# bf16 copies of two weights in DRAM, and a seven-product stage three steps deep, in a hybrid decoder layer

## What is computed

```python
hcat = x @ w_in                                  # conv inputs B, C, h and retention q, k, v, g
y_conv = b_gate * causal_short_conv(c_gate * hc, conv_w)
o = chunkwise_retention(rotary(q), rotary(k) * 128**-0.5, v)
y_ret = silu(g) * head_group_norm(o, ret_gn_w, ret_gn_b)
mix = concat([y_conv, y_ret], -1) @ w_out
x = layer_norm(2**0.25 * x + mix, ln1_w, ln1_b)
ff = square(relu(x @ w_ff1)) @ w_ff2             # 1024 -> 4096 -> 1024
ple = sigmoid(x @ w_ple_gate) * (p @ w_ple_proj)
x = layer_norm(2**0.25 * x + ff + ple, ln2_w, ln2_b)
```

## Time and profile before

| | us |
|---|---|
| median of 6 runs | 813.43 (810.13 to 848.31) |
| the profiled execution | 814.77 |
| span of its slowest core (core 1), all rows from here | 813.2 |
| spans of its cores 0 to 7 | 800.2, 813.2, 800.4, 807.7, 810.1, 803.0, 808.8, 802.8 |
| busy on core 1: PE, DVE, ACT, POOL | 763.5, 545.4, 305.7, 181.5 |

### The profile page before, as it was taken

The page is one execution under the profiler, slowest core; times in us unless marked ns, Lnnn a source line. Parts: engine busy times, 40 slices in busy tenths (PEclk is TensorE's granted clock), DMA queues, the critical chain, the costliest instruction groups (busy, mean ns, idle before and its releaser), DMA issues.

```text
span 813.2 us, 12342 instructions; the slowest of 8 cores (800.2 to 813.2 us)
## 1 busy us (share of the span) xinstructions
PE 763.5 (94%) x3896; PEld 357.5 (44%) x3896; DVE 545.4 (67%) x762; ACT 305.7 (38%) x624; POOL 181.5 (22%) x209
## 2 busy tenths in 40 slices
PE   3999999999999999999969999999898889999994
PEld 1444455555555454444424444454343334444441
DVE  4565855458865888785438876916777667756667
ACT  2222225655466236655522000125665562200431
POOL 9000036563454311120010000000444440000011
PEclk9999999999999999999989999999999999999997
DMA  9997040601115575799999956591595658186422
GB/s 129 167 177 158 27 130 4 102 15 39 53 53 156 89 119 207 174 297 264 213 213 158 227 218 127 170 322 52 167 297 184 210 155 282 54 156 130 138 95 105
DMA packets 31025, 122.65 MB, mean 151 GB/s; under 512 B 3696, under 2 KB 5872, under 8 KB 24560
## 3 DMA queue, kind: packets, MB, share of 16 engines
q0 software_dynamic: 9360, 39.85, 30.6%
q1 hardware_dynamic: 20736, 80.43, 28.2%
q10 hardware_dynamic: 864, 1.57, 0.8%
HBM read 122.89 MB, written 38.80 MB: 199 GB/s over the span
## 4 chain that ended last, share of the span: by engine, by line
PE 74%; DVE 9%; DMA 8%; issue 4%; POOL 2%; ACT 2%; DVEq 0%; SPq 0%; ACTq 0%; POOLq 0%
PE ps L189 72%; DMA s_w<-ring_105 3%; DMA xT_56<-xT 2%; PE ps L193 2%; DVE xacc L207 2%; DVE ps L196 1%; DVE ycat L196 1%; DMA ring_108<-s_w 1%; DMA ring_109<-s_w 1%; POOL lnst L196 1%; DVE lnst L729 0%; DVE eb_132 L196 0%; DVE xacc L196 0%; ACT tR_140 L218 0%; ACT hT L218 0%
## 5 line engine op out<-in xcount | busy, mean ns | idle before, releaser
L196 DVE TENSOR_TENSOR xacc<-xacc,ps 128x512 f32<-128x512 f32 x80 | 53.1, 685 | 53.5 <-PE ps L189 52.0
L196 POOL TENSOR_TENSOR lnst<-lnst,neghalf 128x1 f32<-128x1 f32 x32 | 32.3, 1011 | 245.2 <-DVE lnst L200 194.5
L189 PE MATMUL ps<-ring_106,ycat 128*128 128x512 bf16 x256 | 61.9, 390 | 5.3 <-DVE hT L196 5.3
L189 PE MATMUL ps<-ycat,ring_108 128*128 128x512 bf16 x208 | 49.8, 387 | 4.2 <-DVE ps L196 2.2
L189 PE MATMUL ps<-ycat,ring_109 128*128 128x512 bf16 x208 | 49.1, 384 | 4.0 <-DMA ring_109<-s_w 2.2
L189 PE MATMUL ps<-ring_104,ycat 128*128 128x512 bf16 x224 | 51.4, 379 | 0.0
L218 ACT ACTIVATE ycat<-ps 128x1024 bf16<-128x1024 bf16 x16 | 16.3, 1021 | 90.6 <-PE ps L193 87.7
L196 DVE TENSOR_TENSOR ycat<-hT 128x2048 bf16<-128x2048 bf16 x36 | 43.4, 1222 | 1.5
L189 PE MATMUL ps<-ycat,ring_106 128*128 128x512 bf16 x176 | 42.0, 385 | 0.0
L189 PEld LDWEIGHTS ps<-ring_106,ycat 128*128 128x128 bf16 x256 | 25.4, 100 | 36.6 <-issue 9.0
L189 PE MATMUL ps<-ring_105,ycat 128*128 128x512 bf16 x160 | 37.3, 379 | 0.3 <-DVE ra_80 L196 0.3
(11 more groups left out here) (348 smaller groups left out, 1589.0 us busy)
## 6 DMA issues: line engine op xcount, KB each, us to landing
out<-xacc SPq DMA_DIRECT2D x14, 512.0 KB, 2.9
s_w<-ring_104 SPq DMA_DIRECT2D x10, 512.0 KB, 10.0
s_w<-ring_105 SPq DMA_DIRECT2D x10, 512.0 KB, 12.6
xtmp<-x SPq DMA_DIRECT2D x8, 512.0 KB, 5.2
ring_106<-w_ff POOLq DMA_DIRECT2D x4, 1024.0 KB, 11.0
ring_108<-w_ff POOLq DMA_DIRECT2D x4, 1024.0 KB, 12.5
ring_109<-w_ff POOLq DMA_DIRECT2D x4, 1024.0 KB, 15.8
s_x1f<-xtmp SPq DMA_DIRECT2D x8, 512.0 KB, 10.1
```

Source lines behind the costliest of these rows:

```text
L189: self.P.op("pe", lambda e: e.matmul(out, lhsT=lhsT, rhs=rhs, start=start, stop=stop, skip_group_check=skip), reads, writes)
L196: self.P.op(eng, lambda e: e.tensor_tensor(out=out, in0=in0, in1=in1, op=op), reads, writes)
```

## The change

Three things are changed.

1. Ten DRAM-to-DRAM copies (`copy_bf16`) cast the eight slabs of `w_ff1` and the two of `w_gate` to bf16 in a new scratch tensor `s_wb`, on POOL's queue, one at the end of each step t = 1 to 10 of the retention loop. `load_slab` then loads these slabs from `s_wb`, still on POOL's queue. `gen_w1` no longer stores `M3` and `M4`; `load_pieces` takes them from `s_wb`.
2. `phase_ff1_last` is reordered so that a stage spans three steps: M2, M3, M1 of n, M6 of n-1, M7 of n-2, M5 and M4 of n-1. Banks: r in 0 to 2, t in 3 to 5, p in 6 and 7. `eb` has names of its own, and the slab ring 3 gets new ones afterwards. `load_pieces` stands at other places; the first gate slab's prefetch moves from n = 12 to n = 14.
3. `gen_out` becomes one generator `gen_outs` for all eight blocks, two steps per block: statistics of b, then the output of b-1; the reload of b-1, then the two norm operations of b. One step is issued per stage from n = 2. There is no flush before the second gate: what is left runs in the gate, whose loop steps it until the block it needs has been reloaded.

```diff
-    s_w1 = nc.dram_tensor("s_w1", [4, 7, 128, 4, 512], BF16).ap()
+    s_w1 = nc.dram_tensor("s_w1", [4, 5, 128, 4, 512], BF16).ap()
+    s_wb = nc.dram_tensor("s_wb", [10, 128, 8, 512], BF16).ap()
...
-            h.dma("pool", ring[i][:], wsrc[nm][g], ("ring", i), [], r)
+            src, rd = wsrc[nm][g], []
+            if nm in ("ff1", "gate"):
+                k = g + 8 * (nm == "gate")
+                src, rd = s_wb[k], [("s_wb", k)]
+            h.dma("pool", ring[i][:], src, ("ring", i), rd, r)
+
+        def copy_bf16(k):
+            h.dma("pool", s_wb[k], w_ff1[k] if k < 8 else w_gate[k - 8], ("wc", k // 4, k % 4), [],
+                  [("s_wb", k)])
...
+            if 1 <= t <= 10:
+                copy_bf16((0, 4, 1, 5, 2, 6, 3, 7, 8, 9)[t - 1])
...
-            for m, (t, r) in (("M3", a[0]), ("M4", b[1])):
-                h.dma("sp", s_w1[g, W1.index(m)], t, ("st",) + r[0], r, [("s_w1", g, m)])
...
-                return [(3 * n + k) % 8 for k in range(3)]
+                return n % 3, 3 + n % 3, 6 + n % 2
...
+            def stage(n, split=False):
+                if not split:
+                    first(n)
+                if n >= 3:
+                    last_sums(n - 2)
+                first_sums(n)
+                if n == 0:
+                    xsum("M6")
+                if n == 1:
+                    xsum("M7")
+                if n % 4 == 3:
+                    load_pieces(n // 4 * 7 + 13)
+                if n >= 2:
+                    product(n - 1, "M6", banks(n - 1)[2], True)
+                    sq6 = relu(banks(n - 1)[2])
+                if n >= 2:
+                    product(n - 2, "M7", banks(n - 2)[0], True)
+                    sq7 = relu(banks(n - 2)[0])
+                keep(n)
+                if n >= 2:
+                    square(n - 1, 1, 1, sq6, "act")
+                    square(n - 2, 0, 0, sq7, "pool")
+                if n % 4 == 1 and n > 1:
+                    load_pieces((n // 4 - 1) * 7 + 17)
+                if n >= 2:
+                    bg.step()
+                if n >= 1:
+                    r, t, p = banks(n - 1)
+                    product(n - 1, "M5", t, True)
+                    product(n - 1, "M4", r, True)
+                    sq5, sq4 = relu(t), relu(r)
+                    square(n - 1, 1, 0, sq4, "act")
+                    square(n - 1, 0, 1, sq5, "pool")
+                if n % 4 == 0 and n > 0:
+                    load_pieces((n // 4 - 1) * 7 + 16)
...
-                if n == 12:
+                if n == 14:
                     prefetch(17)
...
+                    while s_ == 1 and loaded[0] <= b:
+                        bg.step()
...
+        def gen_outs():
+            for b in range(9):
+                if b < 8:
+                    g = gen_ln(xacc[:, b, :], ("xa", b), lnt[2], lnt[3], "ln2w", "ln2b", b)
+                    next(g)
+                if b > 0:
+                    h.dma("sp", out[(b - 1) * 128:b * 128, :], xacc[:, b - 1, :], ("outq", b - 1),
+                          [("xa", b - 1)], [("out", b - 1)])
+                    outs.append(("out", b - 1))
+                yield
+                if b > 0:
+                    h.dma("sp", xacc[:, b - 1, :], s_x1f[(b - 1) // 4, ((b - 1) % 4) * 128:((b - 1) % 4 + 1) * 128, :],
+                          ("xl", b - 1), [("s_x1f", 7 + b)], [("xa", b - 1)])
+                    loaded[0] = b
+                if b < 8:
+                    for _ in g:
+                        pass
+                    yield
...
-            bg.flush()
+            if s_ == 0:
+                bg.flush()
```

More of the change, by code:

```diff
@@ L412, in build_nc @@
     xtmp = at("xtmp", [128, 8, D], F32, o_w4, [("xt", b) for b in range(8)])
-    eb = [at("eb%d" % i, [128, 512], F32, o_gs + i * 2 * KB, None) for i in range(4)]
+    eb = [at("eb%d" % i, [128, 512], F32, o_gs + i * 2 * KB, ("eb", i)) for i in range(4)]
+    for k in range(2):
+        P.place(("ring", 3, k, 1), o_gs + k * 4 * KB, o_gs + (k + 1) * 4 * KB)
     xs4 = at("xs4", [128, 4, 512], BF16, o_x1b, "xs4")
@@ L487, in build_nc @@
         SUMS = ("M1", "M3", "M6", "M4", "M7")
+        rname = [[("ring", i, 0), ("ring", i, 1)] for i in range(NR)]
         def load_slab(nm, g, i):
-            r = [("ring", i, 0), ("ring", i, 1)]
+            r = rname[i]
             if nm in SUMS:
@@ L1043, in last @@
[L1043 to L1053, removed]
+                e, q = eb[n % 2], ("eb", n % 2)
@@ L1054, in relu @@
+            def relu(bank):
                 i = rn[0] % 4
@@ L1065, in square @@
                     h.tt(eng, dst, tR[i][:], tR[i][:], ALU.mult, [("tR", i, 1)], rd)
+            def stage(n, split=False):
[33 more added lines that the diff above has]
+                    load_pieces((n // 4 - 1) * 7 + 16)
+                if n == 1:
+                    product(0, "M6", banks(0)[2], True)
+                    square(0, 1, 1, relu(banks(0)[2]), "act")
+                    last_sums(0)
+            for m in ("M3", "M1", "M4"):
+                xsum(m)
             first(0, (0,))
@@ L1069, in phase_ff1_last @@
             first(0, (1, 2))
-            first_sums(0)
             first(1, (1, 2))
[L1072 to L1077, removed]
-            for n in range(2, 16):
[L1079 to L1091, removed]
+            stage(0, True)
+            stage(1, True)
+            for n in range(2, 16):
+                stage(n)
                 if n == 4:
@@ L1094, in phase_ff1_last @@
                     cast(wproj[:], w_proj, "wproj", ("wproj", 1))
-                if n == 12:
+                if n == 14:
                     prefetch(17)
[L1097 to L1101, removed]
+            last_sums(14)
+            r, t, p = banks(15)
+            product(15, "M5", t, True)
+            product(15, "M4", r, True)
+            sq5, sq4 = relu(t), relu(r)
+            last_sums(15)
+            product(15, "M6", p, True)
+            square(15, 0, 1, sq5, "pool")
+            square(15, 1, 0, sq4, "act")
+            for n, m, bank, fh, eng in ((15, "M6", p, 1, "act"), (14, "M7", banks(14)[0], 0, "pool"),
+                                        (15, "M7", r, 0, "pool")):
+                if m == "M7":
+                    product(n, m, bank, True)
+                square(n, fh, fh, relu(bank), eng)
+            rname[3] = [("ring", 3, k, 1) for k in range(2)]
+            bx[0] = 0
             prefetch(22)
@@ L1362, in build_nc @@
             if s_ == 0:
-                for b in range(8):
-                    bg.add(gen_out(b))
+                bg.add(gen_outs())
         P.join("sp", outs)
```

58 lines of the change are left out of this document (24 added, 34 removed).

## The result

The changed kernel takes **791.55 us** (median of 10 runs) where the kernel before took 812.71 beside it on the same chip: ratio 0.9735, 95% interval 0.972 to 0.975. The forecast was 789.4 and the range 784 to 800. The profiled execution took 792.73 (814.77 before), 22.0 us less, where the sum had 25.4. In some executions the cores of one die run longer at a lower granted clock: all ratios here leave those out, the medians do not.

The account below looks back on a forecast made before the run. PE was taken as the bound (74% of the span), so gains lay where PE stands idle: 814.8 - 9.0 (first pair) - 17.4 (second pair) + 0.3 (copies) + 0.7 (moved work) = 789.4 us, range 784 to 800.

Parts of the forecast that it names:

- The first pair: Up to the first gate: lighter DMA traffic ends DVE's wait for a late store, -9.0 us, bounds -4 to -9.6.
- (c): First gate: the store waits behind something other than the removed volume, 5 to 8 us stay, 796 us; chance 0.08.
- (d): Whole kernel: nothing moves, each gain being hidden by a new wait; chance 0.01.
- The second pair: MLP products up to the second gate: three-deep order removes most of 20.7 us lost, -17.4 us, bounds -12 and -19.
- (b): Second pair: DVE becomes the bound at 6.5 us per stage and slow clock returns, 797 us; chance 0.18.
- The copies: Retention steps 1 to 10: ten copies at 7.9 us each, last landing before 230 us; +0.3 us, bounds 0 to 2.
- A transfer that takes nothing from PE costs nothing: Retention loop: premise that the copies' DMA traffic, fitting in the 9.6 us between copies, adds no time.
- (a): POOL's DMA queue: copies delay the MLP slabs; above 12.5 us per copy each us costs ten, 824 us at 16; chance 0.05.
- What moves behind the pair: Second gate: block 7's norm and two outputs move in, last reload some 17 us into it; +0.7 us, bounds 0 to 3.

Follow-up runs that it names:

- the repeat: The changed kernel unaltered, run again beside further variants on one chip: 791.93 us, ratio 0.971 to the kernel before.

## Why the prediction held, step by step

**The first pair: right.** Five blocks of the first gate take 10.8 us on every core for the 20.4 of the earlier trace rows, and core 1 reached the pair 9.9 us earlier. The first-gate wait was a DMA backlog, as read from the earlier trace rows: the store in it lands in 6.6 us for 27.3, and 16 of the 26 us of DMA that I counted as removed would have done. (I had put the store's next use at 402; the wait began at 403.6.) Rivals (c) and (d) fall with it.

**The second pair: the length right, the cause wrong.** 99.7 us came out for 96.8 + 3.3 = 100.1 (16 stages of 6.05; the 7 x 0.86 that I wrote is 6.02). But the prediction made the three-deep order the edit that removes the waits, with the even norms as what frees SP. The runs turn this around. Even norms alone bring the pair from 114.5 to 101.1 us; the order without them leaves it at 108 to 114. I had priced DVE as 5.1 us per stage, half a norm in each, which is a rate. Before, a whole norm came in one piece ahead of `last(n-1)` and `middle(n)`, and it is the longest piece, 5.7 us, that PE had to wait out. Most of the 13 us is this split on DVE: on the two cores where PE waited for no piece, the bursts in the new order cost 10.5 us or more. The freed SP is the smaller part: PE's waits for pieces fell from 3.6 to 0.8 us per core, those for sums from 8.2 to 1.0. The two were not tried apart by an edit. That the time came out near the sum is partly luck: the edit that did most was in the change to serve another. The row was at hand: the waits in the earlier trace rows were for DVE's sums while DVE was 85 of 120 us busy, which is not an engine short of rate. Rival (b) took the same average and fell: DVE was busy 80.6 of 100 us (core 1), and PE waited for it only at the two ends of the pair, 1.3 us in all. Its slow second operation was real, and no matter: 1847 ns on average now for the 1591 of the earlier trace rows.

**The terms do not add.** -9.0 and -17.4 were summed as if each stood alone. Alone the copies gave 3.5 us and the norms 14; copies and norms together gave 21 to 22. The time is that of the slowest core, and the cores that came early out of the first gate lost it again to late pieces as long as SP stood behind outputs and norms. Since all parts were in the change, the sum held.

**The copies: free, at more than my price.** From the third on they queue, and the seven after it land on core 5 between 165.6 and 234.4, (234.4 - 165.6) / 7 = 9.8 us each, above the bound of 7.9 made of a cast load and 1 MiB of writing. The step that failed is to price the transfer by loads, which do not write to DRAM; the last landed at 234.4, not before 230. That the writing is what makes up the difference was not tried. The last copy on core 5, its issue on POOL and its time to landing:

```profile
206.67 0.60 POOL L231 DMA_DIRECT2D s_wb<-w_gate  x1
```
```profile
s_wb<-w_gate POOLq DMA_DIRECT2D x1, 1024.0 KB, 27.7
```

The 10 us per copy and the end at 225 to 235 us that I worked out from the Trainium skill ("DMA: Bandwidth & Descriptors", section "Latency and other measured facts") agree with this trace. But the page's transfers do not cast, and its rates were measured with rows 512 KiB apart (207) and 4 MiB and 4 KiB apart (214); contiguous tiles, as the copies have, it only recommends.

**"A transfer that takes nothing from PE costs nothing": true at ten, false at fifteen.** I expected the victim in the copies' own queue, and rival (a) set the limit at 12.5 us per copy, 125 us of copying (three quarters of its 172 us are 129). Five more copies made it 15 x 9.8 = 147 us, at which (a) expects 789.4 + 22 = 811 from late slabs; 817.7 came, and by another way. SP's loads of x came late. They landed in 2.4 to 3.1 us before, in 19.9 to 53.6 beside ten copies (core 5, 115 to 240 us), and with a median of 78 beside fifteen, where DVE stood 22 us for one (core 6). With ten copies the tightest of these loads lands 19.5 us before DVE first reads it (core 5, 234.6 and 254.1); by 9.8 us per copy two more would use that up, an estimate. The idles of about 1 us near 216 us on two cores, which two of the expectations put down to such a load, are not that: DVE reads none of the reloaded blocks before 245 us. Most runs with ten copies at these steps have such idles on one to four cores, the kernel before on none; their cause stays open.

**What moves behind the pair: the term that missed.** +0.7 with bounds 0 to 3 came out as +4.9 on the slowest core and +1.3 to +2.8 on the rest. It has two parts. 1.3 us are lost on every core, as it seems to the bank numbers of the new order, for which the prediction has no term. For the rest I had the place (SP's four slab loads ahead of the outputs) but took 17 us for the last reload where it needed 26.5, because the first output behind those loads takes 14 us to land, its reload is issued only then, and the next output and the last reload follow one after the other. I had also left out slow matmuls behind the idle, 1.7 us of them on core 5. They need not come: behind an idle of the same 2.71 us on core 4 of the repeat, 63 matmuls took the usual 13.97 (granted clock 1.00). This term is why the sum of 25.4 became 22.0. Swapping the order of issue gave 1.8 us of it back.

## What to carry to other kernels

An engine that is 70 to 80% busy can still be what everyone waits for: look for the longest piece of background work that stands between two of its urgent operations, and split it before reordering anything else. A background transfer is free only if every other queue's small loads still come in time, so look for them in the DMA issues of the same stretch, not just behind it in its own queue. Measure the parts of a change singly and together: where the slowest of several cores counts, a part's gain can be given back in the next stage until another part is there. And where a reordering renumbers buffers, see which one the last operation of a stage holds and which one the next stage takes first.

## What the runs showed of the hardware that I had not expected

- A casting copy of 2 MiB to 1 MiB, DRAM to DRAM, with all eight cores at it, takes 9.8 us in a row; a casting load of the same source added 5.3.
- Small loads on SP's queue stood behind a full POOL queue until it was all but empty: 256 KB landed in 2.4 to 3.1 us before and in up to 53.6 beside it, and on all eight cores seven of the eight loads landed only after the last copy (core 5: copy 234.4, loads 234.6 to 239.1). The lines of DMA issues, core 5, 115 to 240 us, after:

```profile
xin_117<-x SPq DMA_DIRECT2D x1, 256.0 KB, 53.6
...
xin_123<-x SPq DMA_DIRECT2D x1, 256.0 KB, 19.9
```

- Of two idles of PE of 2.71 us at the same place, one was followed by 1.7 us of slow matmuls and the other by none. What decides that stays open.
